# The order of maxima, scaling, exponentials and copies in eight attentions, with two more probability tiles

## The reference

```python
# differential attention, 4 heads: two softmaxes, one subtracted from the other
s = einsum('bqhid,bkhid->bhiqk', q, k) * DA ** -0.5
p = softmax(s, axis=-1)
w = p[:, :, 0] - lam * p[:, :, 1]
ya = rms_norm(einsum('bhqk,bkhd->bqhd', w, v), g_diff) * (1 - lam_init)
# latent attention (MLA), 8 heads: scores of two parts
s = (einsum('bqhd,bkhd->bhqk', qn, kn) + einsum('bqhd,bkd->bhqk', qr, kr)) * MLA_SCALE
yb = einsum('bhqk,bkhd->bqhd', softmax(s, axis=-1), v)
# window attention, 8 heads: context and a band of 3 x 128 keys, with a sink
s_b = where(abs(qpos - kpos) <= WINDOW, s_b, NEG_INF)
p = softmax(concatenate([s_c, s_b, sink], axis=-1))[..., :-1]
yw = p[..., :n_ctx] @ cv + p[..., n_ctx:] @ vn
```

## Time and profile before

| | us |
|---|---|
| median of 3 runs | 4296.6 (4293.11 to 4300.32) |
| profiled execution, its own time | 4292.65 |
| its span | 4290.4 |
| TensorE busy | 3877.8 (90%) |
| VectorE busy | 2250.6 (52%) |
| ScalarE busy | 1584.6 (37%) |
| mean granted TensorE clock | 0.962 of full |

### The profile page before, as it was taken

One profiled execution on the slowest core, in us unless ns is written; L12 is line 12 of the kernel. 1 busy time (PEld: TensorE's weight loads), 2 busy tenths in 40 slices (PEclk: granted clock), 3 DMA queues, 4 the chain that ended last, 5 costly groups with the idle time before them and its releaser, 6 DMA issues. The chain is left out here.

```text
span 4290.4 us, 53699 instructions
## 1 busy us (share of the span) xinstructions
PE 3877.8 (90%) x19922; PEld 3017.7 (70%) x19922; DVE 2250.6 (52%) x3880; ACT 1584.6 (37%) x2699; POOL 317.9 (7%) x282
## 2 busy tenths in 40 slices
PE   4987988998999888988999899979879998988998
PEld 3865566777788787865666688856568886657886
DVE  6345576854554474355722455355645525565552
ACT  2234571112442353245621344233434424353431
POOL 0000001111000000100000100103010010401001
PEclk8999999999999999999999999989899999989999
DMA  4100004552223243200012233212123322202332
GB/s 172 58 29 16 4 2 167 186 190 76 86 98 102 98 158 128 67 25 19 1 66 88 76 98 98 98 66 67 37 69 98 98 95 82 79 17 82 94 100 80
DMA packets 86728, 350.82 MB, mean 82 GB/s; under 512 B 9520, under 2 KB 9648, under 8 KB 85680
## 3 DMA queue, kind: packets, MB, share of 16 engines
q1 hardware_dynamic: 72752, 298.53, 21.3%
q0 software_dynamic: 13824, 50.34, 3.5%
HBM read 346.73 MB, written 2.10 MB: 81 GB/s over the span
## 5 line engine op out<-in xcount | busy, mean ns | idle before, releaser
L493 DVE TENSOR_TENSOR split_low<-weight_ring,split_high 128x1024 fp32r<-128x1024 f32 (+1 forms) x456 | 606.4, 1330 | 890.0 <-ACT split_high L485 875.2
L485 ACT ACTIVATE split_high<-weight_ring 128x1024 fp32r<-128x1024 f32 (+1 forms) x474 | 525.6, 1111 | 1039.3 <-PE banks L1356 468.8
L1484 PE MATMUL banks<-normed_high,split_high 128*128 128x512 f32 (+1 forms) x1760 | 653.7, 371 | 78.0 <-DVE normed_low L432 37.9
L1484 PE MATMUL banks<-normed_low,split_high 128*128 128x512 f32 (+1 forms) x1760 | 650.5, 370 | 0.0
L1484 PE MATMUL banks<-normed_high,split_low 128*128 128x512 f32 (+1 forms) x1760 | 650.4, 370 | 0.0
L1484 PEld LDWEIGHTS banks<-normed_high,split_high 128*128 128x128 f32 x1760 | 334.3, 190 | 139.7 <-issue 84.1
L1484 PEld LDWEIGHTS banks<-normed_low,split_high 128*128 128x128 f32 x1760 | 334.6, 190 | 55.2
L1484 PEld LDWEIGHTS banks<-normed_high,split_low 128*128 128x128 f32 x1760 | 333.9, 190 | 55.9
L1356 PE MATMUL banks<-hidden_high,split_high 128*128 128x512 f32 (+1 forms) x880 | 324.4, 369 | 8.5 <-DVE split_low L493 8.5
L1356 PE MATMUL banks<-hidden_high,split_low 128*128 128x512 f32 (+1 forms) x880 | 323.7, 368 | 0.0
L1356 PE MATMUL banks<-hidden_low,split_high 128*128 128x512 f32 (+1 forms) x880 | 323.7, 368 | 0.0
(11 more groups left out here) (286 smaller groups left out, 6595.6 us busy)
## 6 DMA issues: line engine op xcount, KB each, us to landing
weight_ring<-in_up SPq DMA_DIRECT2D x220, 512.0 KB, 3.5
weight_ring<-in_down SPq DMA_DIRECT2D x80, 704.0 KB, 4.0
modulation_ring<-in_ada POOLq DMA_DIRECT2D x80, 512.0 KB, 4.6
weight_ring<-in_merge SPq DMA_DIRECT2D x48, 768.0 KB, 4.5
weight_ring<-in_inputs SPq DMA_DIRECT2D x36, 512.0 KB, 3.5
weight_ring<-in_out SPq DMA_DIRECT2D x32, 512.0 KB, 3.6
latents<-in_ada POOLq DMA_DIRECT2D x16, 512.0 KB, 4.7
weight_ring<-in_xbc SPq DMA_DIRECT2D x16, 512.0 KB, 3.6
```

The costliest lines, as they stand in the source:

```text
L485: act.activation(k.splits[0][:, (n0 + panel) % RING, 0:width], k.slot(n0 + panel)[:, 0:width], ACT.Copy).then_inc(k.high_ready.sem, 1)
L493: dve.tensor_tensor(k.splits[1][:, s, 0:width], k.ring[:, s, 0:width], k.splits[0][:, s, 0:width].bitcast(F32), ALU.subtract).then_inc(k.l ...
L1484: last = pe.matmul(sums(r, half), w, x, start=(c + j == 0), stop=(c == KT - 1 and j == 2))
```

## The change

The probability tiles become six: the four of `probs` and two spare ones that every call names (turned tiles 2 and 3 in the differential attention, which keeps two turned tiles; two latents tiles in the others; two more branch tiles in the second model). The small columns become six each. Every step now has a mask, so that the branch without one goes; the context steps of the window attention get the zero broadcast. VectorE's and ScalarE's loops are put in another order. TensorE's loop is not edited, except for which semaphore frees the score banks and which tile a turn reads.

```diff
-def attention(k, steps, turned, scratch=None):
+def attention(k, steps, turned, spare, scratch=None):
...
-    sums = k.scalars[:, 32:36]
-    biases, sinks, inverses = (k.scalars[:, 36 + 4 * i:40 + 4 * i] for i in range(3))
+    sums, biases, sinks, inverses = (k.scalars[:, 32 + 6 * i:38 + 6 * i] for i in range(4))
+    tiles = [k.probs[:, s, :] for s in range(4)] + spare
 
     def one(columns, m):
-        return columns[:, m % 4:m % 4 + 1]
+        return columns[:, m % 6:m % 6 + 1]
+
+    def probs(m):
+        return tiles[m % 6][:, 0:steps[m // 2]["keys"]]
...
             def score(t):
                 for j in range(2):
                     if t >= 1:
-                        pe.wait_ge(*scores_free(2 * t + j))
+                        pe.wait_ge(*k.max_ready(2 * t + j - 1))
...
                 dve.wait_ge(*k.scores_ready(m + 1))
-                if step["mask"] is not None:
-                    if t >= 2:
-                        dve.wait_ge(*k.probs_turned(per * (t - 2) + min(j, per - 1) + 1))
...
-                elif sink is None:
...
-                else:
-                    link(dve.tensor_reduce(bias, scores(m, step["keys"]), AX.X, ALU.max, negate=True))
-                    dve.tensor_tensor(bias, bias, sink[j][1], ALU.min).then_inc(k.max_ready.sem, 1)
+                if t >= 3:
+                    dve.wait_ge(*k.probs_turned(per * (t - 3) + min(j, per - 1) + 1))
+                dve.tensor_tensor_reduce(probs(m), scores(m, step["keys"]), step["mask"], -1.0,
+                                         3e38 if sink is None else sink[j][1], ALU.add, ALU.min,
+                                         accum_out=bias).then_inc(k.max_ready.sem, 1)
...
-                if combined and t >= 2:
-                    dve.wait_ge(*k.output_stored(t - 1))
+                if combined and t >= 3:
+                    dve.wait_ge(*k.output_stored(t - 2))
...
             for t in range(U + 2):
+                if t < U:
+                    maximum(t, 0)
+                    maximum(t, 1)
                 if 1 <= t <= U:
                     normalise(t - 1, 0)
                     normalise(t - 1, 1)
-                if t < U:
-                    maximum(t, 0)
-                    maximum(t, 1)
                 if t >= 2:
                     store(t - 2)
...
             for t in range(U + 1):
-                if t >= 1:
-                    copy(t - 1, 0)
                 if t < U:
                     exponential(t, 0)
                     exponential(t, 1)
+                if t >= 1:
+                    copy(t - 1, 0)
                 if t >= 1 and per == 2:
                     copy(t - 1, 1)
...
-    attention(k, steps, turned, scratch=...)
+    attention(k, steps, turned[0:2], turned[2:4], scratch=...)
...
-    attention(k, steps, turned)
+    attention(k, steps, turned, [latents[:, 0, :], latents[:, 1, :]])
...
-                              mixed[:, 8 + r, at:at + P], sink=sink))
+                              mixed[:, 8 + r, at:at + P], mask=k.scalars[:, 14:15].to_broadcast([P, CTX]), sink=sink))
...
-    attention(k, steps, [tile[:, 24 + s, :] for s in range(4)])
+    attention(k, steps, [tile[:, 24 + s, :] for s in range(4)], [tile[:, 28 + s, :] for s in range(2)])
```

More of the change, by code:

```diff
@@ L981, in result @@
         return k.psum[:, 6 + groups[t] % 2, 0:P]
-    def scores_free(m):
-        before = steps[m // 2 - 1]
-        return (k.max_ready if before["mask"] is not None else k.exp_ready)(m - 1)
     with nc.Block() as block:
@@ L1008, in turn @@
                     last = pe.transpose(turning()[0:size, c * P:(c + 1) * P],
-                                        k.probs[:, (2 * t + j) % 4, c * P:c * P + size], k.table("ident"))
+                                        probs(2 * t + j)[:, c * P:c * P + size], k.table("ident"))
                 last.then_inc(k.probs_turned.sem, 1)
@@ L1050, in maximum @@
                 dve.wait_ge(*k.scores_ready(m + 1))
-                if step["mask"] is not None:
-                    if t >= 2:
-                        dve.wait_ge(*k.probs_turned(per * (t - 2) + min(j, per - 1) + 1))
-                    dve.tensor_tensor_reduce(k.probs[:, m % 4, 0:step["keys"]], scores(m, step["keys"]),
-                                             step["mask"], -1.0, 3e38 if sink is None else sink[j][1],
-                                             ALU.add, ALU.min, accum_out=bias).then_inc(k.max_ready.sem, 1)
-                elif sink is None:
-                    dve.tensor_reduce(bias, scores(m, step["keys"]), AX.X, ALU.max, negate=True).then_inc(
-                        k.max_ready.sem, 1)
-                else:
-                    link(dve.tensor_reduce(bias, scores(m, step["keys"]), AX.X, ALU.max, negate=True))
-                    dve.tensor_tensor(bias, bias, sink[j][1], ALU.min).then_inc(k.max_ready.sem, 1)
+                if t >= 3:
[3 more added lines that the diff above has]
+                                         accum_out=bias).then_inc(k.max_ready.sem, 1)
             def normalise(t, j):
                 m, step = 2 * t + j, steps[t]
-                p, total, inverse = k.probs[:, m % 4, 0:step["keys"]], one(sums, m), one(inverses, m)
+                p, total, inverse = probs(m), one(sums, m), one(inverses, m)
                 dve.wait_ge(*k.exp_ready(m + 1))
@@ L1078, in normalise @@
                                                   ALU.mult))
-                    first = k.probs[:, (m - 1) % 4, 0:step["keys"]]
+                    first = probs(m - 1)
                     dve.scalar_tensor_tensor(first, p, inverse, first, ALU.mult, ALU.add).then_inc(
@@ L1113, in exponential @@
                 m, step = 2 * t + j, steps[t]
-                p, bias = k.probs[:, m % 4, 0:step["keys"]], one(biases, m)
+                p, bias = probs(m), one(biases, m)
                 act.wait_ge(*k.max_ready(m + 1))
@@ L1117, in exponential @@
                     act.activation(one(sinks, m), step["sink"][j][0], ACT.Exp, bias=bias)
[L1118 to L1125, removed]
+                act.activation(p, p, ACT.Exp, bias=bias, scale=-1.0, accum_out=one(sums, m)).then_inc(
+                    k.exp_ready.sem, 1)
             def copy(t, j):
@@ L1666, in mix_branches @@
                               square=squares[:, 6 * h + at // P:6 * h + at // P + 1]))
-    attention(k, steps, turned, scratch=rope_queries.rearrange("p a b -> p (a b)").rearrange("p (a b) -> p a b", b=P))
+    attention(k, steps, turned[0:2], turned[2:4], scratch=rope_queries.rearrange("p a b -> p (a b)").rearrange("p (a b) -> p a b", b=P))
     project_latents(k, l, context, mixed, keys, values, latents, rope_queries, squares)
```

## The result

| | before | after |
|---|---|---|
| median us | 4297.94 (4 runs) | 4784.67 (4781.21 to 4788.31, 4 runs) |
| ratio, 95% interval | 1 | 1.1135 [1.112, 1.1149] |
| span of the profiled execution | 4290.4 | 4786.1 |
| mean granted clock | 0.962 | 0.904 |

The kernel became 11.4% slower; 4711 us (4590 to 4850) had been forecast.

What follows compares the result with a forecast made beforehand. Before, the differential loop was bound by scaling, turn, copy and two exponentials, the latent loop by TensorE's work. Forecast: 4292.65 + 269 (new loop) + 145 (clock) = 4707, median 4 us above, so 4711 us; range 4590 to 4850.

Steps and rivals of the forecast that it cites:

- The loop's price: All eight attention calls: new serial loop score, both maxima, scaling, turn makes TensorE idle each step; +269 us (240 to 295).
- The direct signs: Attention calls: TensorE idle before scaling-released turns grown over 200 us, latent step 8.8 us or more, stretches between attentions unchanged.
- costed at nothing: ScalarE's later copy, behind the exponentials: claimed covered in the latent step; if the cover fails, +5 us in all.
- The rival in which the clock holds: Attention calls: the loop's chain is right but TensorE's clock stays steady, 4566 us; chance 0.18.
- The clock's term: TensorE's work in the attention calls slows as idle stretches lower its clock; +145 us, between 0 and about 450.
- The taken clock of 0.79: Clock assumed for the first model's attention calls, from the second model's calls before; +120 us on 453 us of work.
- the forecast's formula: TensorE work between bubbles times (1/clock - 1): 453 us at 0.79 gives +120, second model at 0.65 +12.5 per call.
- the 519 of the rival: Attention calls: chain right, work nearly all at the low clock level, +519 instead of +145, 5085 us; chance 0.07.
- Bubbles: TensorE's idle stretch per attention step: hand-over, two maxima(t), scaling(t-1); 3.55 us differential, 2.73 us latent in layer 2.
- the clock of 0.54: Entry of the second differential call before the change, with a 1.96 us wait: cited as evidence that waits lower the clock.
- no effect: TensorE's work is the same and 90% of the span, so 4297 us; needs score(t+1) ahead of turn(t-1); chance 0.02.
- a faster kernel: Maxima ahead feed exponentials earlier, copy leaves the loop; differential step about 4.1 us, together 4237 us; chance 0.03.

Runs made afterwards that it cites:

- The filled kernel: Changed kernel plus idle TensorE products (2 + keys // 128 per step, half the first filling's number) before the turn, where TensorE waits anyway: 4558.73 us, ratio 1.0601.

## Why the prediction was right, and what was mis-sized

- That the kernel gets slower, and why, held. TensorE's unchanged order puts turn(t-1) behind score(t), VectorE's new order puts the scaling of t-1 behind the maxima of t, and score, maxima, scaling and turn become one line. Undoing VectorE's order alone breaks it (348 us back), undoing ScalarE's alone does not (0 us), and the tiles are no part of it.
- The loop's price held: +269 us forecast at the present clock, 258 (251 to 266) measured in the kernel with filled gaps, 274 as growth of TensorE's idle time. By call (latent and window together) +31, +88, +27, +75, +23 and +22 us against forecasts of 32, 84, 31, 70, 26 and 26.
- The direct signs came: a turn 5.71 us after the score, no change between the calls (3556 us of the span before, 3559 after). TensorE's idle time before turns that a scaling released grew from 60 to 374 us, where more than 200 us more had been named; that before turns that waited for a copy fell from 33 to 7 us, so the copy, costed at nothing, was covered.
- The rival in which the clock holds gave 4566 us. The filled kernel is about that case, made by hand, at 4559 us; in the changed kernel itself the clock did not hold, so the rival is out. Its idle stretches of 2.66 and 3.51 us are followed by matmuls at the lower level, where the 1.47 us of before were not.
- The clock's term was the one mis-sized: +145 us forecast, 226 measured (219 as growth of TensorE's busy time). Two errors, of about equal weight. The taken clock of 0.79 was too high: it was 0.71 to 0.83 in the first model's calls and 0.60 and 0.53 in the second's, where 0.65 was taken. With these measured means the forecast's formula (work x (1/clock - 1)) gives about 180 us. The rest, some 45 us, lies in the formula: it takes the mean clock of a stretch as if the level were spread evenly over idle and busy time. The trace of the changed kernel shows that it was not. In the first model's calls the mean granted clock was 0.87 to 0.95 over TensorE's idle time and 0.61 to 0.77 over its busy time; in the latent step above it was 0.98 in the 2.66 us of idle time and 0.64 in the 4.62 us of turn, weighing and turn behind it. With the clocks of the busy time the formula gives 240 to 250 us, too much by some 20, and that remainder stays open.
- The forecast's 0.79 was borrowed from calls of the kernel before whose idle stretches before a turn were at most 1.27 us, and not derived. That the time fell inside the range although the term was 81 us short is owed to a range wide enough for it.
- Slips in the working, none of which changes the sum. The effect of the clock is said to be at most "about 450" us; that is the first model's 453, and with the second model it is the 519 of the rival (which is the second in the list, and called the third above it). Bubbles "more than double" those of before is true of 3.55 against 1.47 us, not of the latent loop's 2.73. And the clock of 0.54 did not come after the wait of 1.96 us: it was already 0.53 in the score matmuls before that wait (1865.80 to 1868.60), and what went before these were two waits of 0.96 and 1.20 us around 0.87 us of transposes. That wait was thus no evidence of what a wait of such a length does to the clock.
- The rivals of no effect and of a faster kernel fell. The first named its own condition, that score(t+1) stands ahead of turn(t-1). With that condition supplied, and the store out of the way, the differential step became 3.64 us, less than the 4.1 us that the second rival had for it. The gain was real but not in the orders that were changed.

## What to carry to other kernels

Orders of several engines form loops together, so a reorder on one engine is to be read against the unchanged queues of the others: write down, for one step in steady state, the cycle through every queue, and take the longest. Moving one engine a step ahead helps only if the engine that feeds it and the waits queued in front of it (here TensorE's score and VectorE's store) move as well; here half of such a change was worse than none (4785 and 4493 us against 4298). And an idle stretch on TensorE can be priced twice, once as waiting and once in the clock of the matmuls behind it: stretches of 2.66 and 3.51 us in every step were, those of 1.47 us in the first differential call before were not (clock 1.00).

## What the runs showed of the hardware

Idle products in a stretch where TensorE waits anyway bought 226 us: in the half filling, 944 products (1888 matmul instructions, 21810 on the page against 19922) brought the granted clock of the first model's calls from 0.71 to 0.83 up to 0.97 to 0.99. The loss at the lower clock was not random from step to step. In the changed kernel's latent call of layer 2, twelve successive steps took 10.25 to 10.40 us, nearly constant, while the low part shifted from one matmul group to another: over these steps the first turn went from 0.88 to 1.54 us and the second from 1.37 to 0.87. The same step with filling takes 8.78 us.
